# Attention scores per head on two 64-row by 64-column tiles of TensorE's array, in a one-core encoder layer

## The chip, the cores and the metric

The kernel runs on one core of a Trainium2 chip. Its time is the device time of one execution in microseconds (us); the median of several runs is compared. The engines are named as the profile names them: PE (TensorE; PEld is its loading of weights), ACT (ScalarE), DVE (VectorE), POOL (GpSimd) and SP (SyncE, which here issues most DMAs).

## What is computed

Two sequences of 256 tokens with 1024 features go through one layer: a token mixer of three branches (neighbourhood attention, spatial gating, a convolution), and a mixture of 16 experts. Of the reference, the change touches the scores of the neighbourhood attention alone:

```python
qg = q.reshape(B, rows, n_cb, NA_COLS, H, Dh)          # 4 rows, 4 column blocks of 16, 8 heads of 64
kg = k.reshape(B, rows, GRID_W, H, Dh)[:, key_rows[:, None, :, None], key_cols[None, :, None, :]]
s = jnp.einsum('brjqhd,brjwkhd->bhrjqwk', qg * (Dh ** -0.5), kg).astype(jnp.float32) + bias
s = jnp.where(col_valid[:, :, None, :], s, NEG_INF)
p = jax.nn.softmax(s, axis=(-2, -1)).astype(v.dtype)
```

A sequence is a grid of 4 rows by 64 columns. Its queries fall into 4 blocks of 16 columns; a block has 64 queries (4 rows by 16) and sees a window of 32 key columns in all 4 rows, that is, 128 keys.

## The kernel before, in words

All features lie on partitions. Weights come in units of 128 x 1024 f32, numbered u: a DMA by SP (L565), a rounding cast by ACT into `w_hi` (`cast_hi`, L719), the rest by DVE into `w_lo` (`cast_lo`, L1055), and then products on PE in three passes of rounded values (`three`, L1842 to L1844), which make up most of the time. Units 0 to 7 are the convolution's input, 8 to 15 two token-major projections, 16 to 23 queries and keys (an even unit 128 features of queries, an odd one of keys, each two heads, `U_QK`), 24 to 27 the input of the spatial gating, then the gates and branch projections, the output projection, and the experts.

The smaller work is written out by hand between the units, in each engine's program, in an order that depends on u. There are 8 batches of attention, g = 0 to 7: two heads (the pair g // 2) of one sequence (g % 2). In PE's program batch g goes like this:

- `scores(g)` (L1869 to L1881) stands behind unit 18 + g. It waits until its bank is free and the queries and keys of the pair are in SBUF. For each of the 4 column blocks j it makes one f32 product with 128 partitions and 128 stationary columns, `q_pair`, and the 128 keys of the window, `kT`, as the moving operand. The result is 128 rows (head 0's 64 queries, then head 1's) by 128 keys, and the four results fill one PSUM bank.
- `turn(("probsT", g))` (L1837, behind unit 19 + g) transposes the probabilities, having waited for their division by DVE.
- `attend(g)` (L1888, behind unit 20 + g) multiplies them with the values.
- From unit 24 on, the spatial products (L1969) stand between `scores` and `attend`.

In between, DVE adds the bias and the mask (`mask_scores`, L1148, L1152, L1155), ACT exponentiates (`exp_rows`, L771), DVE divides (`divide_probs`, L1159, L1162), ACT copies the transposed probabilities (L779), and both split the attended values (L785, L1169); each of these stands in its engine's program around the casts of some unit.

`q_pair` is block-diagonal. Its column dimension holds, for each block of queries, 64 columns for each head; the rows 0 to 63 (features of head 0) are filled for head 0 alone, the rows 64 to 127 for head 1 alone, and the rest is zero. POOL sets the zeros once (L1724 to L1726), far ahead of the first batch, and PE waits for them before batch 0 (L1876). ACT's `queries(c)` (L753 to L765) fills the rest from PSUM: for each sequence and each of the two heads, one instruction on 64 partitions, with the bias added, so four a pair. Pairs 2 and 3 reuse the buffer of pairs 0 and 1, and wait for their last scores. The keys of a pair need one instruction (`keys`, L750).

Other products that don't fill the array's columns are those of the router, behind the output projection: `router_bias` (L2040) and `route` (L2058) have 16 stationary columns and a full 128 rows. `turn_x1` transposes (L1837) between them.

Of the kernel before, what the change touches and what calls it, by code (L numbers as in the profile page):

```python
# [17 lines left out]
P = 128  # L18
F32 = mybir.dt.float32
# [3 lines left out]
ACT = mybir.ActivationFunctionType  # L23
# [9 lines left out]
GRID = 64  # L33
ROWS = SEQ // GRID
QCOLS = 16
KCOLS = 32
WINDOW = (0, 8, 24, 32)
# [19 lines left out]
LINE = 256  # L57
# [10 lines left out]
V_IN, V_GATE, V_CONVB, V_CVG, V_CVB, V_EMBG, V_EMBB = 0, 28, 52, 56, 60, 64, 72  # L68
# [93 lines left out]
def encoder_layer(nc, A, out_prompt, out_sample):  # L162
# [4 lines left out]
    def sem(name):  # L167
        return ctx.enter_context(nc.semaphore(name))
# [10 lines left out]
    def sb(stack, name, shape, dt=F32, line=32):  # L179
        return stack.enter_context(nc.sbuf_tensor(name, [P] + shape, dt, align_bytes=line))  # L180
# [28 lines left out]
    conv = sb(mix, "conv", [WC, T])  # L209

    early = ExitStack()
    q_pair = sb(early, "q_pair", [2, 2, 4, 2, GRID], F32, LINE)
    kT = sb(early, "kT", [WC, T])
    v_win = sb(early, "v_win", [2, 4, W])
    bias = sb(early, "bias", [WC, 4, P])
# [100 lines left out]
    h = sb(moe, "h", [FF])  # L316
# [46 lines left out]
    x0_normal = sem("x0_normal")  # L363
    x0T_full = sem("x0T_full")
    x0_stored = sem("x0_stored")
    q_blank = sem("q_blank")
    x0T_hi_act = sem("x0T_hi_act")
    x0T_hi_dve = sem("x0T_hi_dve")
    v_stored = sem("v_stored")
# [58 lines left out]
    def bank(name):  # L428
        return psum[banks.at[name][0]]

    def filled(name, i=None):

        b, _, full, unit, units, _, more = banks.at[name]
        if unit is None:
            return psum_full[b], nth(full + 1, more, i)
        return unit_used, nth(unit + 1, units, i)

    def empty(name, i=None):

        b, used, _, _, _, more, _ = banks.at[name]  # L440
        return psum_free[b], nth(used, more, i)

    def drained(name, i=None):

        b, used, _, _, _, more, _ = banks.at[name]
        return psum_free[b], nth(used + 1, more, i)

    def frees(name):
        return psum_free[banks.at[name][0]]

    def fills(name):
        return psum_full[banks.at[name][0]]
# [35 lines left out]
    def tokens_of(t):  # L488
        return slice(t * P, (t + 1) * P)

    def grid(row, seq, col, cols):

        return row[:, seq * SEQ:(seq + 1) * SEQ].rearrange("p (r c) -> p r c", c=GRID)[:, :, col:col + cols]
# [9 lines left out]
    def column(at):  # L503
        return vec[:, at:at + 1]
# [193 lines left out]
    def _(act):  # L698
# [24 lines left out]
        for t in range(TT):  # L723
            act.wait_ge(rstd_ready, t + 1)
            act.activation(x_in[:, t, :], x_in[:, t, :], ACT.Identity, scale=rstd[:, t:t + 1],
                           bias=mu_rstd[:, t:t + 1]).then_inc(x0_normal, 1)
        act.wait_ge(*drained("vectors"))
        for c in range(DC + 1):
            if c < DC:
                if c >= WC:  # L730
# [3 lines left out]
                               bias=column(V_EMBB + c)).then_inc(x0T_full, 1)  # L734
# [18 lines left out]
        def queries(c):  # L753

            act.wait_ge(*filled(("q", c)))
            if c >= 2:
                act.wait_ge(*filled(("scores", 2 * c - 3)))
            for s in range(2):
                tokens = slice(s * SEQ, (s + 1) * SEQ)
                for h2 in range(2):  # L760
                    rows = slice(64 * h2, 64 * h2 + 64)
                    o = act.activation(q_pair[rows, c % 2, s, :, h2, :].rearrange("p j (r c) -> p r j c", r=ROWS),
                                       bank(("q", c))[rows, tokens].rearrange("p (r j c) -> p r j c", j=4, r=ROWS),
                                       ACT.Identity, bias=column(V_IN + c)[rows, :])
            o.then_inc(frees(("q", c)), 1)  # L765

        def exp_rows(g):
# [25 lines left out]
        for u in range(U_MERGE + 1):  # L793
            if u < U_MERGE:
                cast_hi(u + 2)
            if u == U_QK - 1:
                act.wait_ge(x0_stored, 16 * TT)
            if 20 <= u < 28:
                copy_probsT(u - 20)
            if 21 <= u < 29:  # L800
                split_attended(u - 21)
            if u > U_USG:
                gated_chunk_hi(u - U_USG - 1)
            if u < U_V and u % 2:
                glu(u // 2)
            if U_QK <= u < U_USG:
                c = (u - U_QK) // 2
                keys(c) if u % 2 else queries(c)
            if 18 <= u < 26:
                exp_rows(u - 18)  # L810
            if u == U_VSG + 3:
                for t in range(TT):
                    act.wait_ge(*drained(("vsg", t)))
                    act.activation(vs[:, t, :], vs[:, t, :], ACT.Gelu_apprx_tanh).then_inc(vsg_gelu, 1)
            if U_USG <= u < U_MERGE:
                c = u - U_USG
                if c >= 2:
                    act.wait_ge(gated_lo, c - 1)
                act.wait_ge(*filled(("usg", c)))
                act.activation(tmp[:, c % 2, :], bank(("usg", c))[:], ACT.Gelu_apprx_tanh,  # L820
                               bias=column(V_IN + 12 + c)).then_inc(frees(("usg", c)), 1)
# [164 lines left out]
        j = U_MOE + 4 + 12 * 14  # L986
# [32 lines left out]
        with act.register("over_act") as reg:  # L1019
            act.reg_load(reg, overflow[0:1, 0:1])  # L1020
            with act.If(act.snap(reg) > 0):
                act.wait_ge(out_stored, 16 * (TT + 2))
                with act.Fori(0, EXPERTS) as e:
                    for b in range(3):
                        n, j = e * 3 + (EXPERTS + b), U_OVER + 12 * b
# [663 lines left out]
    def _(pool):  # L1689
# [31 lines left out]

        pool.wait_ge(x0_stored, 16 * TT)
        pool.wait_ge(unit_used, 3)
        for h2 in range(2):  # L1724
            other = q_pair[64 * h2:64 * h2 + 64, :, :, :, 1 - h2, :].rearrange("p b s j q -> p (b s j) q")
            pool.memset(other, 0.0).then_inc(q_blank, 1)  # L1726

        pool.wait_ge(var_ready, 2 * TT)
        pool.tensor_tensor(rstd[:], var_eps[:], minus_half[:], ALU.pow).then_inc(rstd_ready, 1)
# [97 lines left out]
    def _(pe):  # L1827
        def open_bank(name, i=None):

            if banks.at[name][1]:  # L1830
                pe.wait_ge(*empty(name, i))
# [37 lines left out]
        def scores(g):  # L1869

            hp, seq = g // 2, g % 2
            open_bank(("scores", g))
            pe.wait_ge(*drained(("q", hp)))
            pe.wait_ge(*drained(("k", hp)))
            if g == 0:
                pe.wait_ge(q_blank, 2)  # L1876
            for j in range(4):
                o = pe.matmul(bank(("scores", g))[:, j * P:(j + 1) * P],
                              q_pair[:, hp % 2, seq, j].rearrange("p h q -> p (h q)"),
                              grid(kT[:, hp, :], seq, WINDOW[j], KCOLS), start=True, stop=True)  # L1880
            o.then_inc(fills(("scores", g)), 1)  # L1881

        def attend(g):
# [57 lines left out]
        for u in range(2, U_MERGE):  # L1941
# [15 lines left out]
            else:  # L1957
                c = u - U_USG
                features(u, [("usg", c)], xT_hi, xT_lo)
            if 18 <= u < 26:  # L1960
                scores(u - 18)
            if u >= U_USG:

                c = u - U_USG
# [3 lines left out]
                for t in range(TT):  # L1968
                    o = pe.matmul(bank(("spatial", c))[:, tokens_of(t)], vs[:, t, c * P:(c + 1) * P], w_sT[:, c, :],  # L1969
                                  start=True, stop=True)  # L1970
# [5 lines left out]
            if 19 <= u < 27:  # L1976
                g = u - 19
# [126 lines left out]
        for k in range(1, TT + 1):  # L2104
            at = EXPERTS * k
            o = pe.matmul(bank("position")[:, at:80], ones_r[:], sel[:, 0:80 - at], start=False, stop=k == TT)
# [95 lines left out]
        j = U_MOE + 4 + 12 * 14  # L2202
# [44 lines left out]
        with pe.register("over_pe") as reg:  # L2247
            pe.reg_load(reg, overflow[0:1, 0:1])
            with pe.If(pe.snap(reg) > 0):
                pe.wait_ge(out_stored, 16 * (TT + 2))  # L2250
                with pe.Fori(0, EXPERTS) as e:
                    for b in range(3):
                        n, j = e * 3 + (EXPERTS + b), U_OVER + 12 * b
# [60 lines left out]
```

## Time and profile before

| | |
|---|---|
| median of 3 runs | 778.81 us (778.55 to 779.31) |
| the profiled execution, its time | 777.9 us |
| the profiled execution, its span | 776.1 us |
| mean granted clock of PE, as a share of the full one | 0.992 |
| PE busy | 745.4 us, 96% of the span |
| DVE busy | 609.9 us, 79% |
| ACT busy | 432.6 us, 56% |
| POOL busy | 72.0 us, 9% |

The span runs from the first to the last instruction of the profiled execution, and times within it are counted from its start. The time of the execution is 1.8 us longer than the span. A matmul's duration in the profile is longer than its share of the time, because matmuls are pipelined: the distance between two starts is what one costs. An f32 product that isn't a transposition shows as two matmuls and two loads.

### The profile page before, as it was taken

To read this page: it belongs to the slowest core of one execution; us is meant where nothing else is said; L and a number is where in the kernel's file an instruction comes from. 1 tells how busy PE (TensorE), PEld (TensorE's weight loads), DVE (VectorE), ACT (ScalarE), POOL (GpSimd) and SP (SyncE) were. 2 spreads that over 40 slices of the span, in tenths; PEclk is the share of its full clock that TensorE was granted. 3 is DMA by queue.
4 is the path that set the end of the run, shared out by engine and by line. 5 is a ranking of instruction groups with operands and counts; after the bars stand their busy time and mean duration, and the time that the engine had idled before them with its cause. 6 is when DMAs were issued, how large, how long until landed. Compare 5 with 4: busy or idle time off the path is not lost.

```text
span 776.1 us, 10638 instructions
## 1 busy us (share of the span) xinstructions
PE 745.4 (96%) x3516; PEld 616.5 (79%) x3516; DVE 609.9 (79%) x827; ACT 432.6 (56%) x585; POOL 72.0 (9%) x96
## 2 busy tenths in 40 slices
PE   4999999999999999999999979999999999999995
PEld 3888877887888888888888857888888888888873
DVE  5799977777678857444348888999999999999977
ACT  5522235657322335422421456888888888888851
POOL 5000000000000000000011121111111111110314
PEclk9999999999999999999999989999999999999998
DMA  9744657232343452332388587999999999999682
GB/s 297 238 98 108 204 147 205 71 93 84 109 134 109 112 167 74 115 103 88 104 303 300 186 302 255 351 392 379 388 386 389 391 400 384 381 394 378 146 171 111
DMA packets 137489, 175.51 MB, mean 226 GB/s; under 512 B 15419, under 2 KB 75559, under 8 KB 137431
## 3 DMA queue, kind: packets, MB, share of 16 engines
q1 hardware_dynamic: 128896, 154.95, 58.8%
q0 software_dynamic: 7616, 19.34, 8.3%
q10 hardware_dynamic: 934, 0.69, 0.3%
q8 instruction: 23, 0.38, 0.2%
q14 instruction: 20, 0.16, 0.1%
HBM read 164.06 MB, written 19.11 MB: 236 GB/s over the span
## 4 chain that ended last, share of the span: by engine, by line
PE 85%; DVE 8%; DMA 2%; ACT 2%; SPq 2%; issue 1%; POOL 0%; DVEq 0%; ACTq 0%; POOLq 0%
PE bank L1842 25%; PE bank L1844 25%; PE bank L1843 25%; DVE w_lo L1055 2%; PE bank L2137 2%; DMA raw<-in_w_in_dram 2%; SPq L606 1%; DVE conv L1125 1%; DVE conv_odd L1125 1%; PE bank L2058 1%; PE bank L1837 1%; PE bank L2152 1%; PE bank L2238 1%; PE bank L1888 1%; PE bank L1904 1%
## 5 line engine op out<-in xcount | busy, mean ns | idle before, releaser
L1055 DVE TENSOR_TENSOR w_lo<-raw,w_hi 128x1024 fp32r<-128x1024 f32 x103 | 125.0, 1220 | 77.2 <-ACT w_hi L719 77.1
L719 ACT CAST w_hi<-raw 128x1024 fp32r<-128x1024 f32 x103 | 107.0, 1048 | 101.5 <-PE bank L1844 97.6
L1842 PE MATMUL bank<-xT_hi,w_hi 128*128 128x512 f32 x352 | 138.5, 393 | 2.7 <-DVE xT_lo L1093 1.5
L1844 PE MATMUL bank<-xT_hi,w_lo 128*128 128x512 f32 x352 | 137.1, 390 | 0.0
L1843 PE MATMUL bank<-xT_lo,w_hi 128*128 128x512 f32 x352 | 137.0, 389 | 0.0
L1842 PE MATMUL bank<-w_hi,xgT_hi 128*128 128x512 f32 x198 | 80.1, 405 | 1.0 <-issue 1.0
L1842 PEld LDWEIGHTS bank<-xT_hi,w_hi 128*128 128x128 f32 x352 | 66.1, 188 | 17.3 <-issue 3.1
L1844 PE MATMUL bank<-w_hi,xgT_lo 128*128 128x512 f32 x198 | 77.5, 391 | 0.0
L1843 PE MATMUL bank<-w_lo,xgT_hi 128*128 128x512 f32 x198 | 77.3, 390 | 0.0
L1844 PEld LDWEIGHTS bank<-xT_hi,w_lo 128*128 128x128 f32 x352 | 66.1, 188 | 14.0
L1843 PEld LDWEIGHTS bank<-xT_lo,w_hi 128*128 128x128 f32 x352 | 66.1, 188 | 13.4
L834 ACT ACTIVATE gate<-bank,vec 128x512 f32<-128x512 f32 x24 | 16.5, 689 | 83.2 <-PE bank L1844 83.2
L1055 DVE TENSOR_TENSOR w_lo<-raw_more,w_hi 128x1024 fp32r<-128x1024 f32 x40 | 48.2, 1221 | 5.7 <-ACT w_hi L719 5.4
L1055 DVE TENSOR_TENSOR w_lo<-raw_late,w_hi 128x1024 fp32r<-128x1024 f32 x40 | 48.2, 1220 | 4.1 <-ACT w_hi L719 3.9
L1125 DVE SCALAR_TENSOR_TENSOR conv<-conv_in,conv_col,conv 128x512 f32<-128x512 f32 x60 | 44.6, 744 | 0.0
L719 ACT CAST w_hi<-raw_more 128x1024 fp32r<-128x1024 f32 x40 | 41.2, 1049 | 4.5 <-PE bank L1844 4.5
L1844 PEld LDWEIGHTS bank<-w_hi,xgT_lo 128*128 128x128 f32 x198 | 37.2, 188 | 7.9
L1842 PEld LDWEIGHTS bank<-w_hi,xgT_hi 128*128 128x128 f32 x198 | 37.3, 188 | 7.8 <-issue 1.2
L719 ACT CAST w_hi<-raw_late 128x1024 fp32r<-128x1024 f32 x40 | 41.2, 1050 | 2.5 <-PE bank L1844 2.5
L1843 PEld LDWEIGHTS bank<-w_lo,xgT_hi 128*128 128x128 f32 x198 | 37.3, 188 | 6.6
L1125 DVE SCALAR_TENSOR_TENSOR conv_odd<-conv_in,conv_col,conv_odd 128x512 f32<-128x512 f32 x56 | 41.6, 744 | 0.0
L1055 DVE TENSOR_TENSOR w_lo<-raw_rows,w_hi 128x1024 fp32r<-128x1024 f32 x32 | 38.3, 1218 | 0.0
(289 smaller groups left out, 1530.9 us busy)
## 6 DMA issues: line engine op xcount, KB each, us to landing
raw_more<-in_w_e_dram SPq DMA_DIRECT2D x48, 512.0 KB, 7.0
raw<-in_w_e_dram SPq DMA_DIRECT2D x48, 512.0 KB, 7.9
raw_late<-in_w_e_dram SPq DMA_DIRECT2D x48, 512.0 KB, 7.1
raw_rows<-in_w_e_dram SPq DMA_DIRECT2D x48, 512.0 KB, 7.9
raw<-in_w_in_dram SPq DMA_DIRECT2D x28, 512.0 KB, 6.5
raw<-in_w_gate_dram SPq DMA_DIRECT2D x24, 512.0 KB, 3.7
y_scratch<-zeros SPq DMA_DIRECT2D x8, 512.0 KB, 5.3
raw<-in_w_o_dram SPq DMA_DIRECT2D x8, 512.0 KB, 3.8
```

Source lines behind the costliest of these rows:

```text
L606: sp.dma_start(v_win[:, seq, j, :], v_grid[:, WINDOW[j]:WINDOW[j] + KCOLS, :]).then_inc(v_windows, 16)
L719: act.copy(hi_slot(j), raw_slot(j)).then_inc(hi_cast, 1)
L834: act.activation(gate[:, n if n < 2 else r % 2, d, :], bank(name)[:], ACT.Sigmoid, bias=column(V_GATE + n * DC + 2 * r + d)).then_inc(free ...
L1055: dve.tensor_tensor(lo_slot(j), raw_slot(j), hi_slot(j).bitcast(F32), ALU.subtract).then_inc(lo_cast, 1)
L1125: o = dve.scalar_tensor_tensor(out=sum_, in0=shifted, scalar=conv_col[:, k, c:c + 1], in1=sum_, op0=ALU.mult, op1=ALU.add)
L1837: o = pe.transpose(bank(name)[:, k * P:(k + 1) * P], tile(k), ident)
L1842: pe.matmul(out, hi_l, hi_r, start=start, stop=False)
L1843: pe.matmul(out, hi_l, lo_r, start=False, stop=False)
L1844: return pe.matmul(out, lo_l, hi_r, start=False, stop=stop)
L1888: o = pe.matmul(bank(("attended", g))[:, j * P:(j + 1) * P], v_win[:, seq, j, hp * P:(hp + 1) * P], probsT[:, j * P:(j + 1) * P], start=Tr ...
L1904: o = pe.transpose(bank(name)[:, tokens_of(t)], x_in[:, t, c * P:(c + 1) * P], ident)
L2137: o = pe.transpose(psum[M_XT + half][:, k * P:(k + 1) * P], xg[:, q, c * P:(c + 1) * P], ident)
```

## The change

The buffer of queries has no zero blocks and is half as large. The copy of queries is one instruction on 128 partitions for each sequence. The memsets and the wait for them are gone. The scores of a block are two products, one for each head: head 0 on rows 0 to 63 of SBUF into partitions 0 to 63 of the bank, head 1 on rows 64 to 127 into partitions 64 to 127, each with 64 stationary columns and 128 moving ones.

```diff
-    q_pair = sb(early, "q_pair", [2, 2, 4, 2, GRID], F32, LINE)
+    qT = sb(early, "qT", [2, 2, 4, GRID], F32, LINE)
...
             for s in range(2):
                 tokens = slice(s * SEQ, (s + 1) * SEQ)
-                for h2 in range(2):
-                    rows = slice(64 * h2, 64 * h2 + 64)
-                    o = act.activation(q_pair[rows, c % 2, s, :, h2, :].rearrange("p j (r c) -> p r j c", r=ROWS),
-                                       bank(("q", c))[rows, tokens].rearrange("p (r j c) -> p r j c", j=4, r=ROWS),
-                                       ACT.Identity, bias=column(V_IN + c)[rows, :])
+                o = act.activation(qT[:, c % 2, s].rearrange("p j (r c) -> p r j c", r=ROWS),
+                                   bank(("q", c))[:, tokens].rearrange("p (r j c) -> p r j c", j=4, r=ROWS),
+                                   ACT.Identity, bias=column(V_IN + c))
             o.then_inc(frees(("q", c)), 1)
...
-        for h2 in range(2):
-            other = q_pair[64 * h2:64 * h2 + 64, :, :, :, 1 - h2, :].rearrange("p b s j q -> p (b s j) q")
-            pool.memset(other, 0.0).then_inc(q_blank, 1)
...
-            if g == 0:
-                pe.wait_ge(q_blank, 2)
             for j in range(4):
-                o = pe.matmul(bank(("scores", g))[:, j * P:(j + 1) * P],
-                              q_pair[:, hp % 2, seq, j].rearrange("p h q -> p (h q)"),
-                              grid(kT[:, hp, :], seq, WINDOW[j], KCOLS), start=True, stop=True)
+                for h2 in range(2):
+                    rows = slice(64 * h2, 64 * h2 + 64)
+                    o = pe.matmul(bank(("scores", g))[rows, j * P:(j + 1) * P], qT[rows, hp % 2, seq, j, :],
+                                  grid(kT[rows, hp, :], seq, WINDOW[j], KCOLS), start=True, stop=True)
             o.then_inc(fills(("scores", g)), 1)
```

## Rows read from the trace of the kernel before

**Rows 1.** The page, sections 1 and 4: PE's busy time, and the chain by engine.

```profile
PE 745.4 (96%) x3516; PEld 616.5 (79%) x3516; DVE 609.9 (79%) x827; ACT 432.6 (56%) x585; POOL 72.0 (9%) x96
...
PE 85%; DVE 8%; DMA 2%; ACT 2%; SPq 2%; issue 1%; POOL 0%; DVEq 0%; ACTq 0%; POOLq 0%
```

**Rows 2.** The list of line L1878: duration in ns, least, median, most.

```profile
L1878 PEld LDWEIGHTS bank<-kT,q_pair x64: 187/192/192, 123.8 to 178.5; 128*128 128x128 f32 x64
...
L1878 PE MATMUL bank<-kT,q_pair x64: 270/275/275, 124.0 to 178.6; 128*128 128x128 f32 x64
...
  DVE probs L1148: 3.4, 5
```

**Rows 3.** Busy time by stretch: PE, PEld, DVE, ACT, POOL (us), clock, DMA.

```profile
139.00:147.00 8.00, 8.00 (x49) 7.02 (x49) 6.14 (x11) 5.95 (x17) 0.00 (x0) 1.00 0.31 91
```

**Rows 4.** Order of time on PE: start, length in us, line, idle time before.

```profile
132.40 0.65 PE L1837 MATMUL bank<-const,probs 128*128 128x128 f32 x4 [0.98 <-DVE probs L1162]
...
189.29 1.16 PE L1888 MATMUL bank<-probsT,v_win 128*128 128x128 f32 x8 [1.79 <-DVE branch_lo L1169]
```

**Rows 5.** The chain that ended last: start, us, engine and line.

```profile
126.13 0.61 DVE probs L1148
...
138.53 0.89 PE bank L1878 x8
...
140.32 0.44 PE bank L1837 x4
...
172.28 1.34 ACT probs L771 x7
```

**Rows 6.** Order of time, PE, around batch 0 (start, length in us).

```profile
123.76 0.39 PE L1844 MATMUL bank<-xT_hi,w_lo 128*128 128x512 f32 x1
...
123.99 1.05 PE L1878 MATMUL bank<-kT,q_pair 128*128 128x128 f32 x8
...
125.11 0.39 PE L1843 MATMUL bank<-xT_lo,w_hi 128*128 128x512 f32 x1
```

**Rows 7.** Line L2058 (ns, as in rows 2), and order of time on PE around it.

```profile
L2058 PEld LDWEIGHTS bank<-x1T,w_routed x64: 92/97/97, 441.8 to 451.3; 128*16 128x16 f32 x64
...
L2058 PE MATMUL bank<-x1T,w_routed x64: 272/273/283, 441.8 to 451.4; 128*16 128x128 f32 x64
...
440.85 1.04 PE L1837 MATMUL bank<-const,x1n_early 128*128 128x128 f32 x8
...
441.81 1.92 PE L2058 MATMUL bank<-x1T,w_routed 128*16 128x128 f32 x16
...
443.67 1.09 PE L1837 MATMUL bank<-const,x1n_late 128*128 128x128 f32 x8
```

**Rows 8.** Line L2040 (ns), and order of time on PE around it.

```profile
L2040 PE MATMUL bank<-vec,w_router_in x16: 163/163/178, 431.2 to 431.6; 128*16 128x1 f32 x16
...
430.85 0.39 PE L1844 MATMUL bank<-w_hi,mT_lo 128*128 128x512 f32 x1
...
431.16 0.55 PE L2040 MATMUL bank<-vec,w_router_in 128*16 128x1 f32 x16
...
431.98 0.39 PE L1843 MATMUL bank<-w_lo,mT_hi 128*128 128x512 f32 x1
```

**Rows 9.** Order of time on DVE, the division of batch 1.

```profile
137.88 0.69 DVE L1162 TENSOR_TENSOR probs<-probs,exp_inv 128x512 f32<-128x512 f32 x1
```

**Rows 10.** ACT: the copies of queries and keys, and the first exponential.

```profile
L762 ACT ACTIVATE q_pair<-bank,vec x16: 468/468/473, 113.3 to 155.4; 64x256 f32<-64x256 f32 x16
...
L750 ACT ACTIVATE kT<-bank,vec x4: 687/687/690, 120.2 to 161.7; 128x512 f32<-128x512 f32 x4
...
127.69 0.40 ACT L771 ACTIVATE probs<-probs,neg_max 128x128 f32<-128x128 f32 x1 [0.29 <-DVE neg_max L1155]
```

**Rows 11.** Order of time on POOL.

```profile
35.95 1.96 POOL L1726 MEMSET q_pair<- 64x1024 f32 x2 [19.17 <-PE bank L1844]
...
134.96 1.04 POOL L1729 TENSOR_TENSOR moments<-moments 128x4 f32<-128x4 f32 x1 [97.06 <-DVE moments L1066]
```

More of the change, by code:

```diff
@@ L365, in encoder_layer @@
     x0_stored = sem("x0_stored")
-    q_blank = sem("q_blank")
     x0T_hi_act = sem("x0T_hi_act")
```

## The prediction

> **What bounds the kernel now.** The page comes first: TensorE (PE) is busy for 745.4 of 776.1 us, and the chain that ended last is 85% PE [rows 1]. So what the change costs or gives on PE counts wherever PE has no slack, and the next question is where the eight score batches lie. The list of line L1878 says: 64 matmuls and 64 weight loads between 123.8 and 178.6 us, two of each per call, as for other f32 products that aren't transposes, and VectorE (DVE) waits for them five times, 3.4 us in all [rows 2]. The table of stretches gives PE 8.00 busy out of 8.00 us from 139 to 147, at a granted clock of 1.00, its 2.4 GHz level [rows 3]. In order of time PE waits twice within the attention part [rows 4]: 0.98 us for the probabilities of batch 0, until 132.40, and 1.79 us for the split of attended values on DVE, until 189.29. These two are cushions.
>
> The chain tells which batches count [rows 5]. The wait at 132.40 ends through DVE and ScalarE (ACT): the mask of scores at 126.13, the exponentials, a cast, the division. Scores 0 is ready at about 125.04 (its first matmul starts at 123.99 and the eight take 1.05 [rows 6]), a microsecond before DVE takes it, so batches 0 and 1 aren't on the path. From 132.40 on the chain is PE back to back, with batches 2 to 5 in it at 0.89 us each and then batch 6. Behind batch 6 it leaves PE: DVE masks, ACT exponentiates (in the chain from 172.28), and a serial chain of the two ends at 189.29. Batch 7 (its last matmul starts at 178.6 [rows 2]) lies beside that chain. So **five batches, 2 to 6, count in full**; 0 and 1 together have 0.98 us to spare, and 7 has the 1.79 us before 189.29. Behind it the long PE stretches follow each other's weights, and a delay goes through to the end.
>
> **The matmuls.** Before, a batch is 8 matmuls at a pace of 0.111 us: (1.05 - 0.275) / 7 [rows 6]; its share of the chain is 0.89. After, each head's product is its own call of 64 rows by 64 columns and still streams 128 columns of keys in two matmuls: 16 instead of 8.
>
> Does a smaller stationary operand stream faster? The trace has no 64-row tile. The nearest row is the router's product L2058, 128 rows by 16 columns of weights against the same 128 f32 columns: its 16 matmuls take (1.92 - 0.273) / 15 = 0.110 each, though its loads are 97 ns instead of 192 [rows 7]. So loading half as many columns gains nothing by itself; streaming sets the pace. I take 0.11 per matmul.
>
> Do the two heads' tiles run side by side? No row shows it. If they do, each still needs its own two matmuls in turn, and issue is in order: head 0's second runs beside head 1's first, head 1's second beside the next window's first. A batch is then 9 steps of 0.11 instead of 8, plus a lag f at each of 7 handovers. Bounds for f: none, or what the closest-packed matmuls here need, L2040 with one moving column: (0.55 - 0.163) / 15 = 0.026 each [rows 8]. I take 0.026, as the only row. The batch is 0.99 + 0.18 = 1.17, against 0.89: **+0.28**; with f = 0 +0.10.
>
> By the Trainium skill, "TensorE: Matmul & The Clock Gate", Part 3 (what overlaps and what doesn't), tiles overlap with about 4 ns between starts while matmuls stay strictly in order; an estimate from that is 0.99 + 0.03 = 1.02 for the batch. No run here shows it yet.
>
> **The change of array shape.** A batch is now surrounded by full-array work, so the array changes shape twice per batch. The trace has such changes around products of 16 columns. Ahead of L2058 eight transposes start at 440.85 at 0.11 each, so their last starts at 441.62; the first L2058 starts at 441.81, 0.08 beyond the pace. The last L2058 starts at 443.46; the next transposes at 443.67, 0.10 beyond it, and those eight take 1.09 instead of 1.04. Sum **0.23** per round trip [rows 7]. L2040 gives a second value: from the L1844 before it to the L1843 behind it 1.13, less two normal intervals of 0.23 (as from 123.76 to 123.99 [rows 6]) and 16 x 0.026, leaves 0.25 [rows 8]. For L1878 the same sum is 125.11 - 123.76 - 0.46 = 0.89, all of it the batch [rows 6], so today nothing is paid. Bounds for 64 by 64: 0 (the shape may not matter) and 0.25. I take 0.23.
>
> So a batch costs 0.28 + 0.23 = **0.51 us more**. Five give 2.57. Batches 0 and 1 give 1.03, of which 0.98 goes into the wait at 132.40: +0.05. DVE gets scores 1 some 0.2 us late, but their division starts at 137.88 and takes 0.69 [rows 9], and PE turns them at 140.32 [rows 5], so that is hidden. Batch 7's 0.51 goes into the wait at 189.29.
>
> **The query copies.** 16 ACT instructions of 64 partitions x 256 elements (0.468 each, 1.9 per pair of heads) become 8 of 128 x 256 [rows 10]. Price of one: between 0.468 (as many elements per partition) and 0.687 (the key copy with 512). I take 0.468, the same free size. That frees some 0.94 us of ACT four times and gains nothing: in the stretch above ACT is busy for 5.95 of 8 us [rows 3], and the queries of pair 0 are copied at 113.3 for a batch at 123.99 [rows 10, 6]. Ahead of the wait at 132.40, too, ACT stood 0.29 us waiting for DVE before the exponentials [rows 10], so an ACT that comes earlier waits longer. With the dearer price, 0.687, the copies still take less than now (1.37 a pair): no loss either.
>
> **The rest.** The two POOL memsets (0.95 each, at 35.95) go; POOL next works at 134.96, after waiting 97 us for DVE [rows 11], and PE's wait for them was long satisfied. Nothing gained, and nothing waits on it. No DMA, queue or other wait is moved; the new calls add no semaphore wait.
>
> **Sum.** 2.57 + 0.05 = +2.6 us on the profiled execution of 777.9 (span 776.1). The median of the three runs is 778.81, 0.9 above the profiled one; with it the forecast is **781.4 us**, 0.33% slower. About 0.2% (1.56 us) is what a measurement of this kernel can tell from no change.
>
> **The rivals.**
> 1. *Cheap overlap.* As above, with f and the change of shape near their lower bounds: 5 x 0.10 = +0.5 at the least, 779.3; with f = 0 and 0.23, +1.65. For it: the prices are from 16-column products, not these. Against: two independent places give 0.23 and 0.25. It counts as "within 0.2%" while a batch costs under 0.31 more.
> 2. *The change doesn't do what it says: no overlap.* Both tiles write the same bank, in different partitions. One after the other, 16 x 0.11 = 1.76, so + 0.87 + 0.23 = +1.10 per batch: five give 5.5, batches 0 and 1 give 2.2 - 0.98 = 1.2, and batch 7 disappears in its cushion. +6.7: 785.5. No row settles it, since no two neighbouring matmuls here use parts of the array that don't overlap; that L1878's loads begin at 123.8, beside the matmul that starts at 123.76, [rows 2, 6] speaks weakly against it, as a sign that the array isn't held as one. Chance 0.16. By the Trainium skill, "TensorEngine Tiling (Array Packing)", Gotcha 1, different row tiles cannot access the same PSUM bank simultaneously, and these two do write one bank; by that rule the forecast would be this case's 785.5. If every change of tile, not only of shape, costs 0.10 too, as the way back to the full array does [rows 7], 7 more per batch make it +1.80: 9.0 + 2.6 = +11.6, 790.4; chance 0.05.
> 3. *Faster.* A tile of half the rows may stream faster than a full one: with overlap and a pace of 0.055, the batch is 9 x 0.055 = 0.50 and, if the change of shape is free, each saves 0.39: -1.95, 776.9. Batches 0 and 1 would add nothing, being ahead of a wait. It decides from a batch, changes of shape included, shorter than 0.58. Against: 0.110 with 16 columns of weights. For: that row has all 128 rows. Chance 0.12, the cases between 0 and -0.2% not counted.
>
> **How the numbers follow.** Overlap at about my prices, slower by over 0.2%: 0.40. Cheap overlap, or a small gain: 0.27. No overlap: 0.16; drained tiles: 0.05; faster: 0.12. Slower 0.40 + 0.16 + 0.05 = 0.61. The likeliest case's own range is 779.3 to 781.9. The range of 8 in 10 leaves out faster by over 0.1% and the drained tiles, and reaches to no overlap: 778.1 to 786.0.
>
> **What would show it.** L1878 with 128 matmuls, with pairs of them starting some 0.03 us apart if they overlap and 0.11 if not; 1.4 us (1.17 + 0.23) from the start of the first score matmul to the next full-array one where it is 0.89 now; the wait at 132.40 gone or nearly so, the one at 189.29 about 0.5 shorter; L762 x8 at 0.47. It is wrong if a batch takes under 1.2 with both changes of shape, if it takes nearly 2, or if the time differs in a stretch without L1878.

## The result, and the profile after

| | before | changed kernel |
|---|---|---|
| median of 11 runs | 778.55 us | 779.98 us |
| ratio, 95% interval | | 1.0017 [1.0009, 1.0025] |
| profiled execution, span | 776.1 us | 778.2 us |

The change costs 1.4 us: it is slower, by less than the 0.2% that the prediction set as its bound. The changed kernel's lines have somewhat smaller numbers: the scores are L1872, the weights' products L1836 to L1838, the query copies L759, the values L1881, the transposes L1831, the mask L1145. The page of the changed kernel, sections 1 and 4:

```profile
PE 747.0 (96%) x3580; PEld 614.5 (79%) x3580; DVE 609.9 (78%) x827; ACT 428.3 (55%) x577; POOL 70.8 (9%) x94
...
PE 82%; DVE 7%; SPq 4%; DMA 3%; ACT 2%; issue 1%; POOL 0%; DVEq 0%; ACTq 0%
```

PE is busy 1.6 us more and ACT 4.3 less; the chain is PE as before. The list of line L1872 of the changed kernel, durations in ns, least, median, most, then idle and waiting time with their counts (before: [rows 2]):

```profile
L1872 PEld LDWEIGHTS bank<-kT,qT x128: 129/133/133, 124.1 to 180.6; 64*64 64x64 f32 x128
L1872 PE MATMUL bank<-kT,qT x128: 269/269/320, 124.1 to 180.7; 64*64 64x128 f32 x128
...
  issue: 2.8, 8
...
  DVE probs L1145: 4.8, 5
```

The copies of the queries, from the list of line L759 (before: [rows 10]):

```profile
L759 ACT ACTIVATE qT<-bank,vec x8: 466/472/475, 113.3 to 155.4; 128x256 f32<-128x256 f32 x8
```

The 64 matmuls have become 128. The idle time "issue" in front of 8 of them is new: 0.35 us ahead of each batch in which PE loads no weights while nothing that the trace shows holds it up. The copies are 8 at 0.472, as priced. PE around batch 2 in order of time, with start and length in us (before, around batch 0: [rows 6]):

```profile
138.57 0.39 PE L1838 MATMUL bank<-xT_hi,w_lo 128*128 128x512 f32 x1
138.89 0.85 PEld L1872 LDWEIGHTS bank<-kT,qT 64*64 64x64 f32 x16 [0.35 <-issue]
138.89 1.09 PE L1872 MATMUL bank<-kT,qT 64*64 64x128 f32 x16
...
139.91 0.97 PEld L1881 LDWEIGHTS bank<-probsT,v_win 128*128 128x128 f32 x8 [0.17 <-issue]
139.91 1.16 PE L1881 MATMUL bank<-probsT,v_win 128*128 128x128 f32 x8
```

The reader is to see four things. From the last full-array matmul to the first of the batch it is 0.32 instead of 0.23. The 16 matmuls need 1.09 - 0.269 = 0.82 from the first start to the last, where 8 needed 1.05 - 0.275 = 0.78. From the last of them (139.71) to the first of the values it is 0.20 instead of 0.11. And those eight take 1.16 instead of the usual 1.06. Sum 0.09 + 0.04 + 0.09 + 0.10 = 0.32 a batch.

The 0.04 isn't the pace of the matmuls either. This is what is under way in the changed kernel in the window from 139.05 to 139.06:

```profile
138.89 0.43 PE L1872 MATMUL bank<-kT,qT 64*64 64x128 f32 x3
```

It ends at 139.32, so the third matmul, 0.269 long, started at 139.05: 0.16 after the first, where a step is 0.11 otherwise. The six steps from there to the last pair fill the other 0.66, at 0.11 each. So all of the 0.32 lies at the two changes of shape: a longer gap ahead of the first matmul and a longer first step behind it, both going in and coming out.

The loading of weights shows one part of it. In the kernel before, in the same place (window from 138.1 to 139.3):

```profile
138.15 0.39 PE L1844 MATMUL bank<-xT_hi,w_lo 128*128 128x512 f32 x1
138.15 1.08 PEld L1878 LDWEIGHTS bank<-kT,q_pair 128*128 128x128 f32 x8
...
139.15 0.30 PEld L1888 LDWEIGHTS bank<-probsT,v_win 128*128 128x128 f32 x2
```

There the first load of the batch began with the last matmul ahead of it, and the values' first load with the last score matmul (139.15). In the changed kernel they begin 0.32 and 0.20 after those matmuls' starts, together with the first matmul that uses them: across a change of shape no weights were loaded ahead.

The chain that ended last of the changed kernel, with start and length in us (before: [rows 5]):

```profile
138.96 1.02 PE bank L1872 x16
...
146.98 1.02 PE bank L1872 x16
...
155.00 1.02 PE bank L1872 x16
```

Further on in the same chain, DVE's mask behind batch 6:

```profile
172.11 0.70 DVE probs L1145
```

The first of the two waits that were cushions, in order of time on PE (before: [rows 4]):

```profile
132.82 0.55 PE L1831 MATMUL bank<-const,probs 128*128 128x128 f32 x3 [0.94 <-DVE probs L1159]
```

And the second:

```profile
191.09 1.16 PE L1881 MATMUL bank<-probsT,v_win 128*128 128x128 f32 x8 [1.32 <-DVE branch_lo L1166]
```

From batch to batch it is 146.98 - 138.96 = 8.02, and again 8.02 to 155.00. In the kernel before it was 7.72, from 138.53 [rows 5] to this row of its chain:

```profile
146.25 0.89 PE bank L1878 x8
```

So **0.30 per batch**; 0.02 of the 0.32 comes back in the products behind the transposes. The granted clock is 1.00 from 139 to 163 in the kernel before and in every variant, so that these distances compare like with like. From the start of the first transposes (the end of the first wait) to the end of the second wait it is 191.09 - 132.82 = 58.27, before 189.29 - 132.40 = 56.89 [rows 4]: +1.38, the whole of the measured difference of 1.4. The rest of the two profiled executions' difference of 2.1 lies ahead of 132 us (0.42: a weight transfer that landed later) and behind 191 (0.3), in stretches without a score batch. The start of these transposes varies among single profiles, whatever the variant: it was 132.82 and, in a second profile of the same changed kernel, 133.99.

### The profile page after: what moved, and what is told of

It is laid out like the page before. It is cut to its first block, busy times and chain, and to the rows that moved or that the text cites. A ratio compares the mean times of both kernels' runs of the same rounds, so it can differ in the third digit from the quotient of the medians.

```text
span 778.2 us, 10755 instructions
## 1 busy us (share of the span) xinstructions
PE 747.0 (96%) x3580; PEld 614.5 (79%) x3580; DVE 609.9 (78%) x827; ACT 428.3 (55%) x577; POOL 70.8 (9%) x94
## 4 chain that ended last, share of the span: by engine, by line
PE 82%; DVE 7%; SPq 4%; DMA 3%; ACT 2%; issue 1%; POOL 0%; DVEq 0%; ACTq 0%
PE bank L1836 24%; PE bank L1838 24%; PE bank L1837 24%; DMA raw<-in_w_in_dram 2%; SPq L582 2%; PE bank L2130 2%; DVE w_lo L1052 2%; SPq L605 1%; PE bank L2051 1%; DMA x_in<-in_x_sample_dram 1%; PE bank L1831 1%; PE bank L2145 1%; PE bank L2231 1%; PE bank L1881 1%; DVE conv L1122 1%
## 5 line engine op out<-in xcount | busy, mean ns | idle before, releaser
L1836 PE MATMUL bank<-xT_hi,w_hi 128*128 128x512 f32 x352 | 138.4, 393 | 3.1 <-DVE xT_lo L1090 1.8
L1838 PE MATMUL bank<-xT_hi,w_lo 128*128 128x512 f32 x352 | 137.1, 389 | 0.0
L1836 PE MATMUL bank<-w_hi,xgT_hi 128*128 128x512 f32 x198 | 80.1, 405 | 1.0 <-issue 1.0
L1836 PEld LDWEIGHTS bank<-xT_hi,w_hi 128*128 128x128 f32 x352 | 66.1, 188 | 18.0 <-issue 3.6
L1838 PE MATMUL bank<-w_hi,xgT_lo 128*128 128x512 f32 x198 | 77.5, 391 | 0.0
L1838 PEld LDWEIGHTS bank<-xT_hi,w_lo 128*128 128x128 f32 x352 | 66.1, 188 | 13.8
L1838 PEld LDWEIGHTS bank<-w_hi,xgT_lo 128*128 128x128 f32 x198 | 37.2, 188 | 7.9
L1836 PEld LDWEIGHTS bank<-w_hi,xgT_hi 128*128 128x128 f32 x198 | 37.2, 188 | 7.8 <-issue 1.2
```

Source lines behind the costliest of these rows:

```text
L1836: pe.matmul(out, hi_l, hi_r, start=start, stop=False)
L1838: return pe.matmul(out, lo_l, hi_r, start=False, stop=stop)
```

## The experiments

The distance from batch to batch in a stretch in which PE never waits is far sharper than the whole time, whose interval is about 0.1% wide on either side. Each experiment is read by both; the distance before is 7.72, in the changed kernel 8.02.

**The loops exchanged (head_outer).** All windows of head 0, then all of head 1.

```diff
-            for j in range(4):
-                for h2 in range(2):
+            for h2 in range(2):
+                for j in range(4):
```

> The changed kernel with the two loops of a score batch exchanged: all four windows of head 0 on one tile, then all four of head 1 on the other. Theory A (the two tiles work side by side, and alternation of tiles is what allows it, each tile taking 0.11 us per matmul): the batch's 16 matmuls take 15 x 0.11 = 1.65 from the first start to the last instead of 0.82, +0.83 per batch, five of them on the path and 0.8 of batches 0 and 1: about +5 us against the changed kernel, 785. Theory B (one small tile alone streams at 0.055 us per matmul, no overlap between tiles): the batch stays at 0.82 and the time at 780.

Measured: 782.61 us, ratio to before 1.0065 [1.0051, 1.0080]; by the ratios that is 3.7 us above the changed kernel, where theory A said about 5. PE around batch 2 in order of time, in head_outer:

```profile
138.38 0.39 PE L1838 MATMUL bank<-xT_hi,w_lo 128*128 128x512 f32 x1
138.69 1.58 PE L1872 MATMUL bank<-kT,qT 64*64 64x128 f32 x16
140.20 1.16 PE L1881 MATMUL bank<-probsT,v_win 128*128 128x128 f32 x8
```

The same kernel's chain:

```profile
138.76 1.51 PE bank L1872 x16
...
147.27 1.51 PE bank L1872 x16
```

The batch takes 1.58 - 0.269 = 1.31 from the first start to the last, and the distance is 8.51. Theory B falls: a small tile alone isn't faster. Theory A holds in kind, and two tiles do work side by side when they alternate. But 1.31 isn't the 15 steps and 1.65 that it wanted. It is 11 steps of 0.11 and twice the 0.05 of a slow first step. If the matmuls started in the program's order, head 1's first could at the earliest start beside head 0's last, and the batch would need 14 steps, 1.64 with the same slow first steps. So head 1's began three steps ahead of that, though all of head 0's stand ahead of them in the program. What is under way in the first hundredth of a microsecond of a batch agrees. In order of time, the changed kernel, of the window from 124.07 to 124.08:

```profile
124.07 0.33 PE L1872 MATMUL bank<-kT,qT 64*64 64x128 f32 x2
```

And the exchanged one, of the window from 138.80 to 138.81, 0.11 after its first start:

```profile
138.69 0.32 PE L1872 MATMUL bank<-kT,qT 64*64 64x128 f32 x1
```

With alternating tiles two matmuls are under way at once from the start; with one tile the first still stands alone 0.11 us later. The durations tell the order. In the list of line L1872 the longest is 320 ns, and these belong to two of a batch's 16 matmuls. In the changed kernel they are the first two to start (window from 138.89 to 138.91):

```profile
L1872 PE MATMUL bank<-kT,qT x2: 320/320/320, 138.9 to 138.9; 64*64 64x128 f32 x2
```

In head_outer the second one to start is an ordinary 269 (window from 138.85 to 138.86), and the other 320 is the sixth (window from 139.18 to 139.19, when the first had ended):

```profile
L1872 PE MATMUL bank<-kT,qT x2: 269/294/320, 138.7 to 138.9; 64*64 64x128 f32 x2
...
L1872 PE MATMUL bank<-kT,qT x4: 269/269/320, 139.0 to 139.2; 64*64 64x128 f32 x4
```

It is so in all eight batches of both. The reading that fits is that 320 marks the first matmul of each tile after a change of shape. Then head 1's first started ahead of head 0's second in the changed kernel, and ahead of head 0's last three in head_outer: a matmul can start on an idle tile ahead of earlier ones that wait for a busy tile. The records don't name the tile, so this order is inferred from the durations and from the 1.31.

**The tiles in the same rows (same_rows).** Head 1's product reads rows 0 to 63 as well, so that its scores, and with them the output, are wrong; the run is read for its time alone.

```diff
-                    o = pe.matmul(bank(("scores", g))[rows, j * P:(j + 1) * P], qT[rows, hp % 2, seq, j, :],
-                                  grid(kT[rows, hp, :], seq, WINDOW[j], KCOLS), start=True, stop=True)
+                    o = pe.matmul(bank(("scores", g))[rows, j * P:(j + 1) * P], qT[0:64, hp % 2, seq, j, :],
+                                  grid(kT[0:64, hp, :], seq, WINDOW[j], KCOLS), start=True, stop=True)
```

> As the changed kernel, but the products for head 1 read rows 0 to 63 too, so that head 1's scores are head 0's; both tiles then lie in the same rows of the array and differ in their columns alone. Theory A, if different columns are enough: 0.82 per batch, 780. Theory A, if the tiles must differ in rows: 1.65 per batch and about 785. Theory B: 0.82.

Measured in the attention part, by the chain:

```profile
139.46 1.02 PE bank L1872 x16
...
147.48 1.02 PE bank L1872 x16
```

The distance is 8.02, as in the changed kernel: different columns are enough for the overlap. The whole took 3124.8 us and says nothing of the change: behind 780 us the program goes on with products on gathered tokens (576 of one form on line L1836), most likely its branch for experts with more tokens than a list holds, since the wrong scores change which experts the tokens go to.

**PE's part alone (pe_alone, pe_alone_again), beside the changed kernel again (after_again).** The buffer with zeros, the 16 copies and the memsets stay.

```diff
-                              q_pair[:, hp % 2, seq, j].rearrange("p h q -> p (h q)"),
-                              grid(kT[:, hp, :], seq, WINDOW[j], KCOLS), start=True, stop=True)
+                for h2 in range(2):
+                    rows = slice(64 * h2, 64 * h2 + 64)
+                    o = pe.matmul(bank(("scores", g))[rows, j * P:(j + 1) * P], q_pair[rows, hp % 2, seq, j, h2, :],
+                                  grid(kT[rows, hp, :], seq, WINDOW[j], KCOLS), start=True, stop=True)
```

> The scores on two tiles as in the changed kernel, but read from the block-diagonal buffer, with the 16 copies, the memsets and the wait for them as before. If all of the change's cost is on PE and the copies give nothing: the same as the changed kernel, 1.4 us above before. If the cheaper copies gave something back: slower than the changed kernel by up to 1 us.

> The two tiles alone once more, with the old copies and memsets. Theory that the cheaper copies give nothing: the same as the changed kernel within the intervals. Theory that they give something: again 0.5 us or more above it.

> The changed kernel once more, beside the next one on the same chip. +1.4 us against before, as the sum over its batches gives (4 x 0.305 + 0.16); interval from 1.0009 to 1.0025.

Measured: pe_alone took 780.51 us, 1.0026 [1.0016, 1.0036]. The two later runs stood beside each other: pe_alone_again 779.48, 1.0010 [1.0000, 1.0019], and after_again, the changed kernel, 780.57, 1.0013 [1.0004, 1.0022]. So the old copies came out 0.5 us above the changed kernel the first time and 1.1 below it the second: no sign of a gain from the new ones, but the whole times alone don't exclude one of half a microsecond. The chain of pe_alone:

```profile
139.47 1.02 PE bank L1880 x16
...
147.49 1.02 PE bank L1880 x16
```

The distance is 8.02 as well. The stretch between the two waits, which holds half of the copies and all of the batches that count, is sharper than the whole times. In the chain of pe_alone it goes from the first to the second of these:

```profile
133.33 0.66 PE bank L1837 x4
...
191.60 1.16 PE bank L1889 x8
```

It is 191.60 - 133.33 = 58.27, with the old copies exactly what the changed kernel has with the new ones. The copies and the memsets gave nothing there, as forecast, and PE's part is the whole cost.

**A change of shape by itself (tiny_tile).** The kernel before, with one more product ahead of each batch, which leaves the output as it is.

```diff
+            pe.matmul(bank(("scores", g))[0:64, 0:1], q_pair[0:64, hp % 2, seq, 0, 0, :],
+                      kT[0:64, hp, seq * SEQ:seq * SEQ + 1], start=True, stop=True)
             for j in range(4):
```

> The kernel before with one more product ahead of each score batch, on a 64 by 64 tile with one moving column, whose result the batch overwrites. It measures the change of shape by itself, at the place of the changed kernel, without the split of the scores. Theory that a round trip of shapes costs a fixed 0.28 us however little is done in it: the distance from one batch to the next grows from 7.72 to about 8.03 (0.28 and two matmuls of 0.026 at most), the same as in the changed kernel, and the time by 1.3 us. Rival (the changed kernel's 0.3 per batch comes from its 16 matmuls): 7.77 and no measurable difference.

Measured: 780.45 us, 1.0023 [1.0008, 1.0037]. PE around batch 2 in order of time, in tiny_tile:

```profile
138.22 0.39 PE L1844 MATMUL bank<-xT_hi,w_lo 128*128 128x512 f32 x1
138.53 0.27 PE L1877 MATMUL bank<-kT,q_pair 64*64 64x1 f32 x2
138.74 1.16 PE L1880 MATMUL bank<-kT,q_pair 128*128 128x128 f32 x8
```

The same kernel's chain:

```profile
138.81 1.09 PE bank L1880 x8
...
146.91 1.09 PE bank L1880 x8
```

The distance is 8.10: +0.38 for two matmuls of a single column. It is more than the forecast 0.31, and more than the changed kernel pays for its whole split batch. Here the tile's own two matmuls come on top of the batch; in the changed kernel the tiled ones stand in place of the full ones. The rival falls: the cost sits in leaving and entering the full array, and is there however little is done in between. From the full array to the tile it is again 138.53 - 138.22 = 0.31, and from the tile's first matmul to the full array's first 0.21; its eight take 1.16, as the ones behind the tiles did in the changed kernel.

**Half the changes of shape (batch_pairs).** Two batches at a time.

```diff
-            if 18 <= u < 26:
+            if 18 <= u < 26 and u % 2 == 0:
                 scores(u - 18)
+                scores(u - 17)
```

> The changed kernel with the batches issued two at a time, behind units 18, 20, 22 and 24, so that the array changes shape 8 times instead of 16. Theory that the fixed cost of about 0.28 us per round trip is what makes the change slower: four round trips go, two or three of them on the path, -0.6 to -0.9 us against the changed kernel, with each pair taking some 0.28 less than two single batches. Rival (the cost is in the matmuls, not in the change of shape): the same time per batch, no gain.

Measured: 779.10 us, 1.0007 [0.9998, 1.0016]. The chain, with two units between these rows:

```profile
139.72 1.89 PE bank L1872 x32
...
155.43 1.90 PE bank L1872 x32
```

It is 15.71 for two units, where two of the changed kernel take 16.04 and two of the one before 15.44. One round trip per two units has gone and with it 0.33; what is left over the kernel before is 0.27, the other round trip. The 16 matmuls more in one piece cost (1.89 - 1.02) / 8 = 0.109 a pair, the pace of the full array's: 32 matmuls on tiles cost what 16 full ones did. In the whole time the gain over the changed kernel is 0.8 us by the ratios, as forecast, but their intervals overlap.

**The values on tiles (attend_tiles, both_tiles).** The split lends itself to the other product of the attention, where a tile also needs only half as many moving columns: the old product also multiplied each head's values with the other head's probabilities, which nothing reads.

```diff
             for j in range(4):
-                o = pe.matmul(bank(("attended", g))[:, j * P:(j + 1) * P], v_win[:, seq, j, hp * P:(hp + 1) * P],
-                              probsT[:, j * P:(j + 1) * P], start=True, stop=True)
+                for h2 in range(2):
+                    at, col = j * P + 64 * h2, hp * P + 64 * h2
+                    o = pe.matmul(bank(("attended", g))[64 * h2:64 * h2 + 64, at:at + 64],
+                                  v_win[:, seq, j, col:col + 64], probsT[:, at:at + 64], start=True, stop=True)
```

> The kernel before with the product with the values (L1888) on tiles instead of the scores: for each window two products of 128 rows by 64 columns with 64 moving columns each, leaving out the half of the old product that nothing reads (the blocks of one head's values with the other's probabilities). If tiles of different columns work side by side, its 16 matmuls of half the length take 0.42 to 0.44 instead of 0.89, less 0.28 for the change of shape: -0.17 per batch, some six on the path, -1.0 us against before, 777.6. If they don't: 16 x 0.055 = 0.88, and +0.28 x 6 = +1.7.

> The changed kernel with the product with the values on tiles as well. Scores and values stand next to each other in units 20 to 23, where the array goes from 64 x 64 to 128 x 64 tiles between them. If that step costs as much as one to the full array: as the changed kernel less what the tiled values give alone, about -1.0. If it is free: 0.1 less again per batch of that stretch, -1.4.

Measured: 778.11 us (the median of 12, one of which took 4293.44), 0.9997 [0.9985, 1.0009], with the values alone, and 778.32, 0.9995 [0.9987, 1.0004], with both. The chain of attend_tiles:

```profile
138.59 0.89 PE bank L1878 x8
...
146.15 0.89 PE bank L1878 x8
```

The chain of both_tiles:

```profile
138.46 1.02 PE bank L1872 x16
...
146.17 1.02 PE bank L1872 x16
```

The distances are 7.56 (-0.16, forecast -0.17) and 7.71 (the same as before). In the whole time neither is told from the kernel before, and the forecast 1.0 us of the values alone is neither shown nor excluded. With both, the scores' 0.30 and the values' -0.16 should add up to 7.86 if nothing were shared; it is 7.71, so a part of the two round trips is shared. The next run tells which.

**One kind of tile for both (column_tiles).** Scores and values on tiles of 128 rows by 64 columns; the zeros of the buffer stay, and the values are changed as above.

```diff
             for j in range(4):
-                o = pe.matmul(bank(("scores", g))[:, j * P:(j + 1) * P],
-                              q_pair[:, hp % 2, seq, j].rearrange("p h q -> p (h q)"),
-                              grid(kT[:, hp, :], seq, WINDOW[j], KCOLS), start=True, stop=True)
+                for h2 in range(2):
+                    rows = slice(64 * h2, 64 * h2 + 64)
+                    o = pe.matmul(bank(("scores", g))[rows, j * P:(j + 1) * P], q_pair[:, hp % 2, seq, j, h2, :],
+                                  grid(kT[:, hp, :], seq, WINDOW[j], KCOLS), start=True, stop=True)
```

> The kernel before, block-diagonal queries kept, with scores and values both on tiles of 128 rows by 64 columns, so that no change of shape lies between the two where they stand side by side. With scores on 64 by 64 and values on 128 by 64 tiles the distance between batches was 7.71. Theory that every change between two shapes costs about 0.14: it goes here, 7.57, as with the values alone on tiles, and 0.7 us less than with both shapes. Rival (a step between two kinds of tiles is free, only the full array is dear): 7.71. If tiles of 128 rows don't overlap with 128 moving columns, 8.4.

Measured: 777.94 us, **0.9988 [0.9979, 0.9997]**, 0.8 us faster than the kernel before, measured beside it. PE around batch 2 in order of time, in column_tiles:

```profile
139.22 1.09 PE L1880 MATMUL bank<-kT,q_pair 128*64 128x128 f32 x16
...
140.03 0.60 PEld L1891 LDWEIGHTS bank<-probsT,v_win 128*64 128x64 f32 x16
140.14 0.63 PE L1891 MATMUL bank<-probsT,v_win 128*64 128x64 f32 x16
```

The same kernel's chain:

```profile
139.29 1.02 PE bank L1880 x16
...
146.85 1.02 PE bank L1880 x16
```

The distance is 7.56, 0.15 below both_tiles. Between the last score matmul (139.22 + 1.09 - 0.273 = 140.04) and the first of the values it is 0.10, without the extra that a change of shape shows, and the values' first load (140.03) again begins beside that matmul. The distances fit one price: some 0.15 for each change between two shapes, and 0.46 saved by the shorter values (7.56 = 7.72 + 0.30 - 0.46 in attend_tiles). The price is a mean: by the starts above, going in costs 0.13 and coming out 0.19. The 0.46, too, is what the fit leaves: the values' 16 matmuls take (0.63 - 0.222) / 7 = 0.058 a pair, so eight pairs 0.47, where eight full ones took 0.89, which is 0.42 less. Two changes and the values give 7.56 here, as measured; three changes, full to 64 by 64 to 128 by 64 to full, give 7.71 in both_tiles, as measured. This is the one version whose interval lies below the kernel before, and only just, out of the seven variants with a right output. Its distance equals that of attend_tiles, so that its lead over that version (0.9997) isn't established.

## Why the prediction came out as it did

The forecast was +2.6 us, 781.4, and slower by over 0.2% was given 0.61. Measured is +1.4, inside the range, and 0.17%, so on the near side of that bound. By the prediction's own mark (a batch under 0.31 more; it was 0.30) what came true is its rival "cheap overlap" (+0.5 to +1.65), which had 0.27, and not the likeliest case with 0.40. A sign that it named for being wrong, a batch under 1.2 with both changes of shape, was just met by the distance: 0.89 + 0.30 = 1.19. That the upper end of the rival, +1.65, is so near is in part luck: it takes nine slots, a free handover and five full batches, where the runs show eight slots, a dearer change of shape and four and a half batches.

- **Which batches count.** Batches 2 to 5 count in full, 8.02 - 7.72 each. Batch 6 counted in full in the forecast, and counted only about half. What goes on from it is DVE's mask (172.11), which starts at its last matmul's end; the way back to the full array comes after that, beside the chain. 4 x 0.30 leaves 0.18 of the 1.38 for the way into it. Batches 0, 1 and 7 vanished in the cushions nearly as forecast: batch 7's wait fell by 0.47, from 1.79 to 1.32, which is batch 7's 0.30 and what batch 6 didn't pay. The wait for the probabilities of batch 0 stayed at 0.94, because the transfer ahead of it landed 0.42 later in this profile; PE itself came to it at 131.88, 0.46 later than before (131.42).
- **The matmuls, +0.28 forecast, +0.04 measured, and that 0.04 a slow first step: this is the step that failed.** The streaming price of 0.11 per matmul of a tile was right (head_outer) and so was the overlap. Wrong was "issue is in order: head 0's second runs beside head 1's first", with its ninth slot and a lag of 0.026 at each handover. The two tiles' matmuls share eight slots from the first one on: 16 in 0.82 from the first start to the last, where the forecast's arrangement needs 0.88 and seven lags of 0.026, 1.06.
- **The order of starts.** By the Trainium skill, "TensorE: Matmul & The Clock Gate", Part 3, the starts of tiles lie 4 ns apart and matmuls keep the program's order. The prediction's estimate from it was 1.02 for the batch; by the same count (first start to last, and one step of 0.11) the trace has 0.93. The short lag agrees with the trace, where the first two matmuls, 0.320 long each, take 0.33 together. Strict order doesn't agree with head_outer: 1.31 instead of 1.64, with a matmul of the second tile started ahead of the last three of the first, as far as the durations tell.
- **The change of shape, 0.23 forecast, 0.28 measured by the same sum** (0.09 going in, 0.09 coming out, 0.10 in the products behind it); with the slow first step of the tiles 0.32. The row of the router product was a good guide though its tile has 16 columns. tiny_tile shows that it doesn't need the split batch, batch_pairs that half of the trips cost half, column_tiles that equal shapes side by side pay nothing.
- **No overlap (0.16).** It fell: 8.02 instead of some 8.8. By the Trainium skill, "TensorEngine Tiling (Array Packing)", Gotcha 1, different row tiles cannot access the same PSUM bank simultaneously; here they did, at different partitions of one bank, without losing time. And the distance is the same when both lie in the same rows (same_rows), so the bank doesn't decide it.
- **Drained tiles (0.05).** It fell: within a batch the tile changes from call to call at the pace of the full array.
- **Faster (0.12).** It fell too: a tile with half the rows streams at 0.11 (the steps of head_outer), not 0.055.
- **ACT and POOL, nothing forecast.** Right: 8 copies at 0.472, ACT 4.3 us less busy, and the same 58.27 from wait to wait with the old copies.

What stays open: why the changes of shape cost what they do. The traces show that no weights are loaded ahead across one, but the profile calls the wait "issue" and names no releaser, and how much of the 0.15 is due to it isn't shown. Open is also whether the 0.35 of idle weight loading ahead of a batch could be filled.

## What to carry to other kernels

Halving a block-diagonal stationary operand into two tiles saves nothing when the moving operand stays as long: the tiles' matmuls run side by side in the time of the full one, and each change of the array's shape costs some 0.15 us. It can gain where the split also shortens the moving operand, as with the values here (-0.46 for +0.30, seen in the distance and not in the whole time), and where products of the same tile shape stand next to each other. For changes of a tenth of a per cent, read the distance between two equal marks in a stretch where the bounding engine never waits; here it told in one profile what 11 timed runs left open. It holds for that stretch alone.

## What the runs showed of the hardware that was not expected

- A round trip out of the full array costs some 0.30 us (8.02 against 7.72); with two one-column matmuls added in it, it is 0.38 (tiny_tile: 8.10).
- Weights for the next product are loaded beside the last matmul of the one before when both have one shape (138.15 before, 140.03 in column_tiles), and not across a change of shape (idle 0.35 and 0.17 in the changed kernel).
- 16 matmuls on two alternating tiles take 0.82 from the first start to the last, 8 on the full array 0.78; the 0.04 is in the first step.
- With the tiles one after the other the batch took 1.31 and not the 1.64 of strict order: by their durations, the second tile's matmuls began ahead of the last three of the first.
- A step from 64 by 64 to 128 by 64 tiles costs 0.15 (7.71 against 7.56), though no full-array work lies between.
